# An expert loop's row gathers without an upper bound: empty slots read zero rows

## The chip, the cores and the metric

The kernel runs on one core of one Trainium2 chip. The metric is the device time in microseconds. Engines are called as in the profile: PE (TensorE), DVE (VectorE), ACT (ScalarE), POOL (GpSimd), SP (SyncE); sixteen DMA engines move the data.

## What is computed

One layer of a streaming encoder on 512 tokens of width 1024: attention, pooling, cross attention, then a mixture of 32 experts of which each token takes 4. Only the last part bears on the change:

```
logits = hf @ w_router + b_router
top_val, top_idx = top_k(logits, 4);  gates = softmax(top_val)
for each expert e, for its tokens:
    gu  = x @ w_gu[e] + b_gu[e]                      # 1024 -> 2048
    act = glu * sigmoid(1.702 * glu) * (lin + 1)      # glu, lin: clamped halves of gu
    y   = act @ w_down[e] + b_down[e]                 # 1024 -> 1024
    out[token] += gate * y
```

All data is fp32. Products are made from split operands (a high part and a low part of fp32r), so every weight unit of 128 x 2048 passes through ACT (high part, L1115) and DVE (low part, L1549) before PE uses it.

## The kernel before

The dense layers run first, to about 650 us. Then all 32 experts are served in turn. The first two are experts 0 and 1, the others follow by falling number of tokens. The first 17 blocks have 96 slots (`CAP`, heavy), the other 15 have 64 (`SLOTS_L`, light); tokens beyond that would go to extra blocks, which run in a loop at the end if there are any.

**Tables.** `hf_rows` in device memory holds the 512 normed token rows and behind them `CAP` = 96 rows of zeros. `slot_table` holds for each slot and block a token index and a gate. It starts with the index 512 + slot and the gate 0, so a slot that gets no token points at a zero row of its own. POOL fills in the tokens by indirect DMA (L772) and loads it as `slots`.

**The loop.** From turn 3 on light and heavy turns alternate. A turn i does the gate/up product of one expert and the down product of the one before it: 12 weight units of 1 MB (8 gate/up, 4 down), which SP loads into six raw buffers. SP waits for a buffer by `lo_done`, DVE's count of finished units. In order of use:

- SP: load unit (L480 gate/up, L487 down);
- ACT: high parts (L1115), and between them the copies of PSUM (`low`, L1145 and L1150; `ybuf`, L1157 and L1165), the gate (L1120) and the high parts of the activations;
- DVE: low parts (L1549), the clamp of the gate half (L1583, once in each turn), the clamp of the other half (L1585), their product (L1591);
- PE: gate/up products (L2273 heavy, L2219 light), down products (L2297, L2243), transposes of the gathered rows `xg` (L2175) and of the activations (L2184), and in light blocks the sums of shifted rows (L2191, L2198), which wait for ACT's `low`.

**POOL.** In each turn POOL issues one gather, for the expert whose gate/up product comes in the next turn: it waits until PE has turned the last rows out of `xg`, copies one column of `slots` to `idx_cur` (L670), and issues the indirect DMA (L675). Then it copies the index and gate column to `ycur` (L696), waits for `ybuf`, and issues the scatter that adds an expert's result rows to `moe_rows` (L702). Gather and scatter share POOL's DMA queue (q0). The scatter has a bound check too: an index above 511 is left out. The first three gathers of the program are written apart: L709 (twice) and L765 (once); their indices come from a product with a selection matrix, so an empty slot has index 0, and they have no bound. `xg` has 96 rows; a light block's gather fills the first 64. The last light turn also issues a gather for block 32, the first extra block.

Of the kernel before, what the change touches and what calls it, by code (L numbers as in the profile page):

```python
# [34 lines left out]
T = 512  # L35
# [127 lines left out]
def build(nc, A, out):  # L163
    with ExitStack() as ctx:
        def at(name, kb, shape, dt=F32):
            return nc.alloc_sbuf_tensor_at(name, shape, dt, offset=SB0 + int(kb * KB))
# [12 lines left out]
        def sem(name):  # L179
            return ctx.enter_context(nc.semaphore(name))  # L180
# [99 lines left out]
        def later(name, shape, dt=F32):  # L280
# [10 lines left out]
        idx_cur = at("idx_cur", 182.75, [CAP, 1], I32)  # L291
# [123 lines left out]
        idx_copied, gathered, x_turned, x_hi, x_ready = (  # L415
            sem(n) for n in ("idx_copied", "gathered", "x_turned", "x_hi", "x_ready"))
# [124 lines left out]
        def _(pool):  # L541
# [122 lines left out]
            def gather(block_column, copied, turned_before, n=CAP):  # L664


                pool.wait_ge(table_in, 16)

                pool.wait_ge(x_turned, turned_before)
                g.tensor_copy(idx_cur[:, :], slots[:, bass.ds(block_column, 1), 0]).then_inc(idx_copied, 1)  # L670

                pool.wait_ge(rows_filled, 16 * (TT + 2))
                pool.wait_ge(hf_stored, 16 * TT)
                pool.wait_ge(idx_copied, copied)
                g.indirect_dma_start(out=xg[0:n, :], out_offset=None, in_=hf_rows,  # L675
                                     in_offset=bass.IndirectOffsetOnAxis(ap=idx_cur[0:n, :], axis=0),
                                     bounds_check=T - 1, oob_is_err=False).then_inc(gathered, 16)

            def select(sel, e, ready, biased=None, used=None, n=CAP):

# [72 lines left out]
            for j in range(1, (T - 1 - SLOTS_L) // CAP + 1):  # L753
# [3 lines left out]
                if j < (T - 1 - SLOTS_L) // CAP:  # L757
# [8 lines left out]
                                 in_offset=bass.IndirectOffsetOnAxis(ap=idx_cur[:, :], axis=0)).then_inc(gathered, 16)  # L766
# [16 lines left out]
            select(sel_gu, third_expert, sel_gu_ready, gu_biased, 2)  # L783
            select(sel_dn, 1, sel_dn_ready, dn_biased, 1)
            gather(3, 2, 3, L)
            add_rows(0, 1)
            select(sel_dn, third_expert, sel_dn_ready, dn_biased, 2)

            def light_turn(i, first=False):
                e = expert_at(i)  # L790
                select(sel_gu_l, e, sel_gu_ready, gu_biased, i + 0, L)
                gather(i + 1, i + 0, i + 1)
                add_rows(i - 2, i - 1, 16 * i - 32, CAP if first else L)
                select(sel_dn_l, e, sel_dn_ready, dn_biased, i + 0, L)

            def heavy_turn(i):
                e = expert_at(i)
                select(sel_gu, e, sel_gu_ready, gu_biased, i + 0)
                gather(i + 1, i + 0, i + 1, L)
                add_rows(i - 2, i - 1, 16 * i - 32)  # L800
                select(sel_dn, e, sel_dn_ready, dn_biased, i + 0)
# [1572 lines left out]
```

## Time and profile before

| | |
|---|---|
| time, three runs | 1771.12, 1771.86, 1773.82 us; median 1771.86 |
| span of the profiled execution, first to last instruction | 1771.6 us, 22444 instructions |
| own time of the profiled execution | not listed apart; its span of 1771.6 us is within 0.3 us of the median of the runs |
| busy | PE 94%, PE weight load 74%, DVE 76%, ACT 63%, POOL 35% |
| mean granted clock of PE | 0.973 of full speed |
| data moved | 493.11 MB, of it 459.30 MB by SP's queue and 28.05 MB by POOL's |

The page cuts the span into 40 slices of 44.3 us. A digit is a busy share in tenths. The expert loop takes slices 17 to 39. A row of a timeline gives the start, the duration, the engine, the line and what it did; in square brackets stands the idle time before it and what ended that. In a row of windows the last three numbers are the granted PE clock (1.00 is full speed), the share of the sixteen DMA engines' time, and GB/s.

### The profile page before, as it was taken

How to read it: one execution, taken by the hardware profiler on the slowest of the kernel's cores; microseconds unless marked ns; L12 is line 12 of the kernel's file. 1: busy time of each engine (PE TensorE's matmuls, PEld its weight loads, DVE VectorE, ACT ScalarE, POOL GpSimd, SP SyncE). 2: the span in 40 equal slices, each digit the busy share in tenths (PEclk: the TensorE clock that was granted, in tenths of full speed). 3: DMA queues.
4: the chain of work that ended last, by engine and by line, in shares of the span. 5: the costliest groups of instructions: out<-in, count | busy, mean ns of one | idle time of the engine just before them, and what ended most of it. 6: DMA issues, size and time to landing. Idle time of an engine off the chain costs nothing.

```text
span 1771.6 us, 22444 instructions
## 1 busy us (share of the span) xinstructions
PE 1659.1 (94%) x7739; PEld 1309.1 (74%) x7739; DVE 1342.7 (76%) x1184; ACT 1121.9 (63%) x1030; POOL 614.6 (35%) x480
## 2 busy tenths in 40 slices
PE   6999999999989889999999999999999999999993
PEld 5877767889866677877777777777777777777772
DVE  5444563335433669999999999999999999999992
ACT  4134564234233245777887887887887887887882
POOL 5002231000000016345455455455454455455442
PEclk9999999999999989999999999999999999999996
DMA  9221222324431238999999999999999999999993
GB/s 316 104 95 60 76 68 83 126 95 143 166 98 48 77 132 303 397 393 383 393 389 398 396 394 397 395 394 397 394 392 395 392 396 396 389 394 397 388 377 105
DMA packets 110114, 493.11 MB, mean 278 GB/s; under 512 B 10461, under 2 KB 10530, under 8 KB 77194
## 3 DMA queue, kind: packets, MB, share of 16 engines
q1 hardware_dynamic: 98752, 459.30, 66.2%
q0 software_dynamic: 9824, 28.05, 6.0%
q10 hardware_dynamic: 1482, 5.01, 0.7%
q8 instruction: 35, 0.57, 0.1%
q14 instruction: 21, 0.17, 0.0%
HBM read 476.44 MB, written 20.38 MB: 280 GB/s over the span
## 4 chain that ended last, share of the span: by engine, by line
PE 39%; DVE 25%; issue 16%; DMA 12%; ACT 7%; POOL 0%; SPq 0%; DVEq 0%; ACTq 0%; POOLq 0%
DVE wlo L1549 18%; DMA raw<-in_w_gu 8%; PE ps L1820 7%; PE ps L1822 7%; PE ps L1821 7%; ACT whi L1115 4%; PE ps L2219 3%; DMA raw<-in_w_down 3%; PE ps L1943 2%; PE ps L1945 2%; PE ps L1947 2%; DVE glu L1583 1%; PE ps L2273 1%; PE ps L1970 1%; DVE lin L1585 1%
## 5 line engine op out<-in xcount | busy, mean ns | idle before, releaser
L1549 DVE TENSOR_TENSOR wlo<-raw,whi 128x2048 fp32r<-128x2048 f32 x380 | 846.9, 2282 | 44.5 <-ACT whi L1115 43.7
L1115 ACT ACTIVATE whi<-raw 128x2048 fp32r<-128x2048 f32 x380 | 714.6, 1912 | 101.7 <-DMA raw<-in_w_gu 51.4
L701 POOL TENSOR_TENSOR mark<-ident 1x1 f32<-1x1 f32 x32 | 160.2, 5007 | 380.1 <-ACT ybuf L1157 209.7
L1275 DVE TENSOR_TENSOR wlo<-raw,whi 128x2048 fp32r<-128x2048 f32 x52 | 120.0, 2331 | 145.6 <-ACT whi L847 145.6
L702 POOL DMA_INDIRECT moe_rows<-ybuf,ycur x32 | 174.4, 5450 | 6.3 <-issue 6.3
L2273 PE MATMUL ps<-whi,xhi 128*128 128x512 f32 x544 | 152.5, 403 | 0.6 <-DVE xlo L1554 0.3
L2273 PE MATMUL ps<-whi,xlo 128*128 128x512 f32 x544 | 146.4, 391 | 0.0
L2273 PE MATMUL ps<-wlo,xhi 128*128 128x512 f32 x544 | 146.4, 391 | 0.0
L847 ACT ACTIVATE whi<-raw 128x2048 fp32r<-128x2048 f32 x52 | 98.0, 1917 | 70.6 <-DVE branch L1426 30.2
L2219 PE MATMUL ps<-whi,xhl 128*128 128x512 f32 x480 | 134.8, 403 | 5.8 <-DVE xhl L1559 5.8
L2219 PE MATMUL ps<-wlo,xhl 128*128 128x512 f32 x480 | 134.4, 404 | 0.0
L2273 PEld LDWEIGHTS ps<-whi,xhi 128*128 128x128 f32 x544 | 101.7, 190 | 24.0 <-DVE wlo L1549 1.2
L2273 PEld LDWEIGHTS ps<-wlo,xhi 128*128 128x128 f32 x544 | 102.8, 189 | 21.9
L2273 PEld LDWEIGHTS ps<-whi,xlo 128*128 128x128 f32 x544 | 102.7, 189 | 21.7
L2219 PEld LDWEIGHTS ps<-whi,xhl 128*128 128x128 f32 x480 | 88.7, 190 | 30.7 <-issue 11.6
L2219 PEld LDWEIGHTS ps<-wlo,xhl 128*128 128x128 f32 x480 | 93.8, 196 | 20.6
L1120 ACT ACTIVATE glu<-glu 96x1024 f32<-96x1024 f32 (+1 forms) x32 | 33.9, 1061 | 92.1 <-DVE glu L1583 92.1
L2297 PE MATMUL ps<-whi,ahi 128*128 128x512 f32 x272 | 87.9, 405 | 0.0
L2297 PE MATMUL ps<-wlo,ahi 128*128 128x512 f32 x272 | 84.5, 392 | 0.0
L2297 PE MATMUL ps<-whi,alo 128*128 128x512 f32 x272 | 83.9, 390 | 0.0
L2243 PE MATMUL ps<-whi,ahl 128*128 128x512 f32 x240 | 76.9, 401 | 0.0
L2243 PE MATMUL ps<-wlo,ahl 128*128 128x512 f32 x240 | 73.9, 389 | 0.0
(383 smaller groups left out, 3020.7 us busy)
## 6 DMA issues: line engine op xcount, KB each, us to landing
raw<-in_w_gu SPq DMA_DIRECT2D x256, 1024.0 KB, 10.1
raw<-in_w_down SPq DMA_DIRECT2D x128, 1024.0 KB, 8.3
raw<-in_w_in SPq DMA_DIRECT2D x14, 1024.0 KB
raw<-in_w_gate SPq DMA_DIRECT2D x8, 1024.0 KB
raw<-in_w_xkv SPq DMA_DIRECT2D x8, 1024.0 KB
raw<-in_w_attn_up SPq DMA_DIRECT2D x4, 1024.0 KB
raw<-in_w_out SPq DMA_DIRECT2D x4, 1024.0 KB
raw<-in_w_xq SPq DMA_DIRECT2D x4, 1024.0 KB
```

Of the source, the lines that this page charges most:

```text
L701: g.tensor_tensor(mark[:, 0:1], ident[0:1, 0:1], ident[0:1, 1:2], ALU.add)
L702: g.indirect_dma_start(out=moe_rows, out_offset=bass.IndirectOffsetOnAxis(ap=ycur[0:n, 0:1], axis=0), in_=ybuf[0:n, :], in_offset=None, co ...
L1115: s.activation(his[m % DEPTH], raws[m % RAWS], ACT.Copy).then_inc(hi_done, 1)
L1275: v_.tensor_tensor(wlo[:, u % RING, :], raw[:, u % RING, :], whi[:, u % RING, :].bitcast(F32), ALU.subtract).then_inc(lo_done, 1)
L1549: v_.tensor_tensor(los[m % DEPTH], raws[m % RAWS], his[m % DEPTH].bitcast(F32), ALU.subtract).then_inc(lo_done, 1)
L1820: t_.matmul(dst, first[0], second[0], start=start, stop=False)
L1821: t_.matmul(dst, first[0], second[1], start=False, stop=False)
L1822: return t_.matmul(dst, first[1], second[0], start=False, stop=stop)
L2219: mm = t_.matmul(ps[:, n, :], xhl[:, k, :], w[:, n * 512:(n + 1) * 512], start=False, stop=False)
L2243: mm = t_.matmul(ps[:, 4 + n, :], ahl[:, k, :], w[:, c:c + 512], start=False, stop=False)
L2273: mm = t_.matmul(ps[:, n, :], a[:, k, :], w[:, n * 512:(n + 1) * 512], start=False, stop=k == KT - 1 and a is xlo)
L2297: mm = t_.matmul(ps[:, 4 + n, :], a[:, k, :], w[:, c:c + 512], start=False, stop=k == KT - 1 and a is alo)
```

## The change

The gathers in the loop lose their bound check. An index above 511 is no longer left out; the DMA reads the row of zeros at that index into `xg`. The three gathers ahead of the loop and the scatter stay as they are.

```
@@ gather(block_column, copied, turned_before, n=CAP)
                 g.indirect_dma_start(out=xg[0:n, :], out_offset=None, in_=hf_rows,
-                                     in_offset=bass.IndirectOffsetOnAxis(ap=idx_cur[0:n, :], axis=0),
-                                     bounds_check=T - 1, oob_is_err=False).then_inc(gathered, 16)
+                                     in_offset=bass.IndirectOffsetOnAxis(ap=idx_cur[0:n, :], axis=0)
+                                     ).then_inc(gathered, 16)
```

## Rows read from the trace of the kernel before

**Rows 1.** The page: slices of the DMA, and the scatter's group.

```profile
DMA  9221222324431238999999999999999999999993
GB/s 316 104 95 60 76 68 83 126 95 143 166 98 48 77 132 303 397 393 383 393 389 398 396 394 397 395 394 397 394 392 395 392 396 396 389 394 397 388 377 105
...
L702 POOL DMA_INDIRECT moe_rows<-ybuf,ycur x32 | 174.4, 5450 | 6.3 <-issue 6.3
```

**Rows 2.** Waits from 938.2 to 1071.3 us: total, times, longest.

```profile
DVE wlo L1549 <- ACT whi L1115: 6.3, 9, 2.5
...
ACT whi L1115 <- DMA raw<-in_w_gu: 5.7, 10, 1.3
```

**Rows 3.** Timeline of DVE: L1583 in eight turns.

```profile
792.49 1.21 DVE L1583 TENSOR_SCALAR glu<-ps 64x1024 f32<-64x1024 f32 x1
...
925.58 1.21 DVE L1583 TENSOR_SCALAR glu<-ps 64x1024 f32<-64x1024 f32 x1
...
1027.18 1.21 DVE L1583 TENSOR_SCALAR glu<-ps 96x1024 f32<-96x1024 f32 x1
...
1058.59 1.21 DVE L1583 TENSOR_SCALAR glu<-ps 64x1024 f32<-64x1024 f32 x1
...
1092.50 1.21 DVE L1583 TENSOR_SCALAR glu<-ps 96x1024 f32<-96x1024 f32 x1
...
1126.41 1.21 DVE L1583 TENSOR_SCALAR glu<-ps 64x1024 f32<-64x1024 f32 x1
...
1457.76 1.21 DVE L1583 TENSOR_SCALAR glu<-ps 64x1024 f32<-64x1024 f32 x1
...
1590.73 1.21 DVE L1583 TENSOR_SCALAR glu<-ps 64x1024 f32<-64x1024 f32 x1
```

**Rows 4.** Timelines of PE and ACT in two light turns; windows with PE's clock.

```profile
1038.28 0.67 PE L2191 MATMUL ps<-low,shift 128*64 128x512 f32 x2 [1.02 <-ACT low L1150]
...
1102.04 1.91 ACT L1115 ACTIVATE whi<-raw 128x2048 fp32r<-128x2048 f32 x1 [1.33 <-DMA raw<-in_w_gu]
...
1105.04 0.67 PE L2191 MATMUL ps<-low,shift 128*64 128x512 f32 x2 [2.45 <-ACT low L1150]
...
1039.00:1043.00 4.00, 4.00 (x24) 3.32 (x23) 4.00 (x3) 3.14 (x3) 0.00 (x0) 1.00 1.01 395
...
1106.00:1109.40 3.40, 3.40 (x13) 2.71 (x12) 2.71 (x3) 2.82 (x2) 0.00 (x0) 0.52 1.02 408
```

**Rows 5.** POOL's queue, 740-757, 776-790, 1118-1123, 1123-1130, 1700-1712 us: packets, MB, share.

```profile
q0 software_dynamic: 112, 0.23, 7.0%
...
q0 software_dynamic: 112, 0.21, 7.6%
...
q0 software_dynamic: 80, 0.24, 24.4%
...
q0 software_dynamic: 80, 0.24, 10.7%
...
q0 software_dynamic: 123, 0.00, 0.6%
```

**Rows 6.** POOL's queue over two stretches, 805.1-938.2 and 1470.4-1603.3 us.

```profile
q0 software_dynamic: 768, 2.39, 7.4%
...
q0 software_dynamic: 768, 1.89, 6.0%
```

**Rows 7.** The gathers by line (ns min/median/max), landing, one issue, PE's use.

```profile
L675 POOL DMA_INDIRECT xg<-hf_rows,idx_cur x30: 1019/1348/3020, 724.9 to 1695.1; - x30
...
DMA to landing us min/median/max: 7.2/8.7/10.0
...
L709 POOL DMA_INDIRECT xg<-hf_rows,first_idx x2: 934/1018/1103, 656.2 to 662.4; - x2
...
1093.54 1.03 POOL L675 DMA_INDIRECT xg<-hf_rows,idx_cur  x1 [0.91 <-POOL idx_cur L670]
...
1118.04 0.88 PE L2175 MATMUL ps<-ident,xg 96*128 96x96 f32 x8
```

## The prediction

> **What bounds the kernel now.** I read the page first [rows 1]. The gathers in question run from 724.9 to 1695.1 us [rows 7], in the expert loop, and there every slice has the DMA engines at 9 tenths and about 395 GB/s. On the same page PE, DVE and ACT stand at 7 to 9 tenths in these slices; such a page names no bound, so the next view is the waits of one stretch of four turns (two light, two heavy) [rows 2]. In 133.1 us ACT waits 5.7 us for gate/up weights to land and DVE waits 6.3 us for ACT. So weights do arrive late at some places, and more DMA traffic could cost time.
>
> The third view is the start of L1583, once in each turn [rows 3]. From 1027.18 to 1058.59 one turn takes 31.41 us; from 1092.50 to 1126.41 the same kind of turn (light) takes 33.91. The pattern repeats every four turns, and the four-turn period is what I cost the change against. The two light turns differ by 2.50 us, and [rows 4] shows why. In the slow one ACT waits 1.33 us for a gate/up unit (1102.04), so its copy of `low` (L1150) is late, PE pauses 2.45 us at L2191, and in the stretch right behind the pause the granted clock is 0.52, that is the lower level, 1.2 GHz; in the quick one PE pauses 1.02 us and the clock stays at 1.00. So the loop is one closed cycle of DMA, ACT, PE and clock; a late weight unit is paid for in every second light turn.
>
> **What the change touches.** Before, a slot without a token holds the index 512 + slot; the bound is 511, so the gather leaves that row out. After, the index is legal (the table has 608 rows) and a row of 4,096 bytes is read. How does a left-out row look now? The last gather of the loop, at 1695.1 us, is for the expert behind the 32nd and has 96 empty slots: from 1700 to 1712 us the pool queue shows 123 packets and 0.00 MB [rows 5]. So a left-out row is a tiny packet, 0.6% of 16 engines in 12 us over 123 packets = 9.4 ns of one engine.
>
> How many rows are added? Blocks 0 to 16 have 96 slots and the 15 others 64: 2,592 slots. Tokens fill 512 x 4 = 2,048 of them (the page has 32 scatters by L702 [rows 1], so no token went to an extra block); 544 are empty. The first three gathers (L709, L765) have no bound already. The scatters of the first two experts move 0.23 and 0.21 MB [rows 5], 56 and 51 rows of 96, so 40 + 45 empty slots lie there; the third expert is the fullest of the rest and I count it full. That leaves 459 rows, and the 96 of the last gather: 555 rows, 2.27 MB, 0.5% of the page's 493 MB.
>
> The price of one row. From 1123 to 1130 us the pool queue holds one light gather alone: 80 packets, 0.24 MB (59 rows), 10.7% of 16 engines in 7 us = 11.98 us of one engine; less 21 tiny packets, 200 ns per row [rows 5]. Added per row: 200 - 9 = 191 ns of one engine, or 11.9 ns of all sixteen. The dearest row of this size in the trace is the scatter's, 24.4% of 5 us for 59 rows, 331 ns, or 20.1 ns of all sixteen [rows 5]; I take the gather's since it is the same operation, and keep the other for the range. If nothing hides them: 459 x 11.9 = 5.5 us (9.2 at the scatter's price), and 96 x 11.9 = 1.1 us for the last gather. The lower bound is nothing.
>
> How much passes through to the span? The trace holds an experiment on this already, since experts are served by falling load. From 805.1 to 938.2 us the pool queue moved 2.39 MB, from 1470.4 to 1603.3 only 1.89 MB [rows 6]: 0.50 MB or 122 rows fewer, half gathered and half scattered. Unhidden that would be 61 x 11.9 + 61 x 20.1 = 1.95 us. The four turns took 925.58 - 792.49 = 133.09 us and 1590.73 - 1457.76 = 132.97 us [rows 3]: 0.12 us, a share of 6%. Four turns hold 640 slots, gathered and scattered together, so 57 to 179 are empty in these stretches, half of them gathered: after the change each moves 28 to 90 rows more, so its pool traffic lies mostly inside what the loop has carried already (461 to 583 rows), and the first two or three stretches lie up to 40 rows above it. By the share of 6% the 459 rows cost 0.3 us; since that share is unproven above 583 rows I take twice this, 0.6 us. What hides the rest is the other work of the cycle: most of ACT's waits for weights fall where DVE is still busy with earlier units. If this cover were gone the cost would be the 5.5 us above.
>
> The last gather is counted at nothing too: its data lands in `xg`, which nobody reads, and all that it can delay is the last few down units, which pass through at the same 6%. Without that cover it is 1.1 us, in the range.
>
> Is a gather itself late? It takes 7.2 to 10.0 us from issue to landing [rows 7]. The one issued at 1093.54 is in `xg` by about 1103.5; PE turns it (L2175) at 1118.04: 14.5 us to spare, against some 0.3 us for 20 to 30 more rows. Nor is POOL late: on it ycur (L696) stands behind the gather and waits for the scatter before it anyway. On POOL the gather takes a median of 1348 ns with the bound against 934 to 1103 without (L709) [rows 7]. I count that at nothing: its results have the 14.5 us, and the fastest bounded one took 1019 ns too. If it were on the path it would be worth up to 30 x 0.33 = 10 us, which is the faster rival's room.
>
> The sum: the profiled execution's span is 1771.6 us, the runs' median 1771.86. 1771.86 + 0.6 = 1772.5 us.
>
> **A rule of the skill against it.** The Trainium skill, DMA: Bandwidth & Descriptors, section Specifications, gives about 358 GB/s as what HBM gives one core. By it this loop is over its limit already and every byte must cost: an estimate from that page is 2.27 MB / 358 GB/s = 6.3 us. The trace disagrees, with slices of 395 GB/s and more [rows 1], and the measurement decides; yet that the traffic has no headroom is just what the first rival says in rows.
>
> **Rivals.** *A, the DMA is the bound and every added row counts.* For it: DMA share full in every slice of the loop, ACT's waits for weights. Against it: the 0.12 us where 1.95 were due. It gives 5.5 us, 1777.3; with the last gather or the dearer price up to 1781. It decides once the pool queue moves more than the cycle carries, and only the first stretches go past what was seen.
>
> *B, the cycle tips to the slow turn.* If the added rows (up to 31 in one gather, 0.4 us) delay weights in the quick light turns as well, PE's pause there grows from 1.02 to 2.4 us, the clock falls there too, and each costs 2.50 us more. There are 7 such turns, one between each two slow ones and one behind: 1771.9 + 17.5 = 1789.4 us. The point is a weight unit 1.3 us later than now, and 122 rows more or fewer did not move the pattern. One such turn more would be 2.5 us, still inside 0.2%. The Trainium skill, TensorE: Matmul & The Clock Gate, section What's actually happening, says that the default state is throttled and that activity releases it; the clock after the long pause agrees.
>
> *C, faster.* A gather without the bound check leaves POOL up to 0.3 us sooner, so its packets and the scatter's are over before the unit on which ACT waits at 1102.04. If that wait goes, so do the long pause and the low clock: 7 slow light turns in the loop (one in 133 us, from 838 to 1638 us), each 2.50 us, 17.5 us in all, 1754. The point is the whole wait of 1.33 us; against it, the gather ahead of that wait took 1.03 us as it is [rows 7], and its rows grow.
>
> *D, nothing changes in the queue*, because the zero rows are left out in some other way: 1771.9, inside the forecast.
>
> **How the numbers follow.** This kernel tells 0.2% (3.5 us) from no change. Forecast with D 0.70 (1772.5, own range 1770.5 to 1775), A 0.16, B 0.07, C 0.07. A and B end slower, C faster; of the forecast's 0.70 a hundredth each way falls outside 0.2%. So faster 0.08, same 0.68, slower 0.24. The range takes in the forecast's spread and A at the gather's price: 1770.2 to 1777.6, leaving out B, C and the dear end of A.
>
> **What would show it.** Pool queue: the packets over the loop stay the same in number, 2.3 MB more, the tiny ones gone where the gathers are; the last gather shows 0.39 MB. L1583 four turns apart: 133.0 to 133.3 us; A says 133.4 to 134.1. PE's pauses at L2191 still alternate between 1.0 and 2.4 us; B and C say that they don't. Wrong would be the prediction if the pattern of pauses changes, or if a gather's row is much dearer than 200 ns, as all gathers then read the same few rows.

## The result, and the profile after

The changed kernel takes 1778.73 us (median of 5 runs, 1775.6 to 1780.46), the kernel before 1771.86 (5 runs). The ratio is 1.0033 with a 95% interval from 1.0020 to 1.0046, that is 5.8 us slower (3.5 to 8.1). The forecast was 1772.5 us, range 1770.2 to 1777.6, with 0.68 on no difference. The time lies outside the range, on the side and near the size of rival A.

How many rows were added can be read from the page alone, in the line of packets. First the line of the kernel before:

```profile
DMA packets 110114, 493.11 MB, mean 278 GB/s; under 512 B 10461, under 2 KB 10530, under 8 KB 77194
```

And the slices, packets and queues of the changed kernel's page, which answer to [rows 1]:

```profile
span 1777.5 us, 22414 instructions
...
DMA  9221212324431238999999999999999999999993
GB/s 323 95 95 60 79 65 84 124 95 142 166 98 48 85 139 305 396 389 384 397 389 398 401 387 398 396 391 401 395 393 401 395 392 398 400 389 389 402 361 104
DMA packets 110114, 495.37 MB, mean 279 GB/s; under 512 B 9909, under 2 KB 9978, under 8 KB 77194
```

The packets are as many as before, but 10461 - 9909 = 552 tiny ones have become rows, and the data has grown by 2.26 MB. The rate in the loop (slices 17 to 39) is about what it was: 384 to 402 GB/s, with one slice of 361, against 377 to 398 before. More bytes at the same rate is what a loop bound by its transfers looks like; the experiments below say how far that holds.

The timeline of DVE has the starts of L1583, which answer to [rows 3]:

```profile
793.15 1.21 DVE L1583 TENSOR_SCALAR glu<-ps 64x1024 f32<-64x1024 f32 x1
...
926.77 1.21 DVE L1583 TENSOR_SCALAR glu<-ps 64x1024 f32<-64x1024 f32 x1
...
1060.54 1.21 DVE L1583 TENSOR_SCALAR glu<-ps 64x1024 f32<-64x1024 f32 x1
...
1460.66 1.21 DVE L1583 TENSOR_SCALAR glu<-ps 64x1024 f32<-64x1024 f32 x1
...
1595.07 1.21 DVE L1583 TENSOR_SCALAR glu<-ps 64x1024 f32<-64x1024 f32 x1
...
1694.99 1.21 DVE L1583 TENSOR_SCALAR glu<-ps 96x1024 f32<-96x1024 f32 x1
...
1729.02 1.21 DVE L1583 TENSOR_SCALAR glu<-ps 64x1024 f32<-64x1024 f32 x1
```

Over four turns that is 133.62, 133.77 and 134.41 us; the prediction had 133.0 to 133.3, and rival A 133.4 to 134.1. For the last two turns the kernel before has:

```profile
1692.20 1.21 DVE L1583 TENSOR_SCALAR glu<-ps 96x1024 f32<-96x1024 f32 x1
...
1723.04 1.21 DVE L1583 TENSOR_SCALAR glu<-ps 64x1024 f32<-64x1024 f32 x1
```

Set side by side, the 5.9 us between the two spans lie in these places:

| stretch | before | after | difference |
|---|---|---|---|
| up to the start of the loop's pattern | 792.49 | 793.15 | 0.66 |
| from there to the last full turn | 899.71 | 901.84 | 2.13 |
| the last turn, in which the empty last gather lands | 30.84 | 34.03 | 3.19 |
| behind it, to the end of the span | 48.53 | 48.43 | -0.10 |

So more than half is in one turn. These are two single executions. In the runs that list both, the span is 1.7 to 1.9 us less than the time, so the one before took some 1773.4 us, which is over its median. The 2.13 us of the second row are less sure than they look: with the last gather's rows alone added (below), where the loop up to there is that of the kernel before, the same stretch takes 898.20 us, 1.51 less than before. The last turn is steadier, as shown below. Here are PE and ACT of the changed kernel in that turn, and a window behind PE's pause:

```profile
1704.68 1.91 ACT L1115 ACTIVATE whi<-raw 128x2048 fp32r<-128x2048 f32 x1 [1.49 <-DMA raw<-in_w_gu]
...
1707.69 0.83 PE L2191 MATMUL ps<-low,shift 128*64 128x512 f32 x2 [2.67 <-ACT low L1150]
...
1708.00:1711.40 3.40, 3.40 (x10) 2.66 (x9) 2.71 (x2) 3.37 (x2) 0.00 (x0) 0.51 1.02 410
```

The kernel before had no wait for weights there, a pause of 1.03 us and the full clock. In the changed kernel a gate/up unit comes 1.49 us late, PE pauses 2.67 us and the clock falls to its lower level. What took the DMA's time is in the queue. From 1700 to 1712 us, where [rows 5] has 123 packets with 0.00 MB and 0.6% of the engines' time, the pool queue of the changed kernel has:

```profile
q0 software_dynamic: 112, 0.39, 10.4%
```

That is the last gather: 96 rows, 208 ns of one engine each. In the other turns the pattern of pauses is no longer strict, which the prediction had named as a sign of being wrong. Two of the long ones are shorter, one comes in a turn that was quick before (1573.70), and the turn behind it, slow before, is quick (1639.79):

```profile
972.51 0.68 PE L2191 MATMUL ps<-low,shift 128*64 128x512 f32 x2 [1.83 <-ACT low L1150]
...
1506.21 0.67 PE L2191 MATMUL ps<-low,shift 128*64 128x512 f32 x2 [1.66 <-ACT low L1150]
...
1573.70 0.68 PE L2191 MATMUL ps<-low,shift 128*64 128x512 f32 x2 [2.42 <-ACT low L1150]
...
1639.79 0.68 PE L2191 MATMUL ps<-low,shift 128*64 128x512 f32 x2 [0.98 <-ACT low L1150]
```

The gather itself has become shorter on POOL and is in time, as [rows 7] had it before:

```profile
L675 POOL DMA_INDIRECT xg<-hf_rows,idx_cur x30: 950/958/3024, 725.4 to 1695.9; - x30
...
DMA to landing us min/median/max: 7.4/8.4/10.3
```

The step from a median of 1348 ns to 958 is not the price of the check. In the run with the last gather's rows alone the check is there as before, and the median is 1029:

```profile
L675 POOL DMA_INDIRECT xg<-hf_rows,idx_cur x30: 1014/1029/3027, 724.2 to 1692.9; - x30
```

The shortest gathers take 1012 to 1019 ns with the check in all but two of the runs, and 947 and 950 in the two without it. So the check takes POOL about 0.07 us; the medians of the runs with it lie anywhere from 1028 to 1737 ns.

### The profile page after: what moved, and what is told of

Its sections match the earlier page's. It is cut to its first block, busy times and chain, and to the rows that moved or that the text cites. A ratio compares the mean times of both kernels' runs of the same rounds, so it can differ in the third digit from the quotient of the medians.

```text
span 1777.5 us, 22414 instructions
## 1 busy us (share of the span) xinstructions
PE 1661.1 (93%) x7739; PEld 1309.1 (74%) x7739; DVE 1344.0 (76%) x1184; ACT 1123.0 (63%) x1030; POOL 599.2 (34%) x480
## 2 busy tenths in 40 slices
DMA packets 110114, 495.37 MB, mean 279 GB/s; under 512 B 9909, under 2 KB 9978, under 8 KB 77194
## 4 chain that ended last, share of the span: by engine, by line
PE 36%; DVE 24%; issue 16%; DMA 14%; ACT 8%; ACTq 0%; POOL 0%; DVEq 0%; SPq 0%; POOLq 0%
DVE wlo L1549 17%; DMA raw<-in_w_gu 9%; PE ps L1820 7%; PE ps L1821 7%; PE ps L1822 7%; ACT whi L1115 5%; DMA raw<-in_w_down 4%; PE ps L1943 2%; PE ps L1945 2%; PE ps L1947 2%; DVE glu L1583 2%; PE ps L2219 1%; PE ps L2273 1%; PE ps L1970 1%; DVE lin L1585 1%
## 5 line engine op out<-in xcount | busy, mean ns | idle before, releaser
L702 POOL DMA_INDIRECT moe_rows<-ybuf,ycur x32 | 170.1, 5316 | 6.1 <-issue 6.1
L2219 PEld LDWEIGHTS ps<-wlo,xhl 128*128 128x128 f32 x480 | 93.8, 195 | 20.6
L1120 ACT ACTIVATE glu<-glu 96x1024 f32<-96x1024 f32 (+1 forms) x32 | 33.9, 1060 | 88.6 <-DVE glu L1583 88.6
```

The source lines that it names most:

```text
L702: g.indirect_dma_start(out=moe_rows, out_offset=bass.IndirectOffsetOnAxis(ap=ycur[0:n, 0:1], axis=0), in_=ybuf[0:n, :], in_offset=None, co ...
L2219: mm = t_.matmul(ps[:, n, :], xhl[:, k, :], w[:, n * 512:(n + 1) * 512], start=False, stop=False)
```

## Experiments

All were timed against the kernel before, each on the same chip as it. Differences in us are the ratio's, times 1771.

**The check or the rows?** One number of the kernel before decides which indices are left out, so the number of rows can be set while the instructions and the number of packets stay (110,114; at a bound of 0 one register move of POOL less per gather).

```
-                                     bounds_check=T - 1, oob_is_err=False).then_inc(gathered, 16)
+                                     bounds_check=T + CAP - 1, oob_is_err=False).then_inc(gathered, 16)
```

> The kernel before with the bound at 607 instead of 511: the check stays, but every zero row is read, 552 rows or 2.26 MB more, as in the changed kernel. Theory T1 (the rows cost: the loop is at the limit of its DMA) and theory T2 (rows beyond what the loop's cycle carries cost, rows fewer gain little) both expect the changed kernel's time, 1776 to 1780 us. Theory T3 (the missing check costs, by the timing of POOL's instructions) expects the time of before, 1771 to 1773.

Measured: 1.0033 (1.0020 to 1.0046), 1777.41 us. That is the changed kernel's ratio to the last digit. With the check and all the rows the time is that of the changed kernel: the rows make the difference, and the missing check shows no effect within these intervals of some 2.3 us either way.

**Other numbers of rows.** The same number at 575 (`T + SLOTS_L - 1`), 383, 255 and 0. The last three leave out rows of tokens too, so those kernels don't compute the whole result.

> The bound at 575: of the empty slots those below 64 are read, that is all of the light blocks (159 rows in the loop) and 64 of the last gather; the heavy blocks' empty slots stay out. T1 expects 159 x 11.9 ns = 1.9 us and up to 0.8 for the last gather: 1773.8 to 1774.6. T2 expects between 0 and 1 us, 1772 to 1773, since the pool queue then stays within what the loop had carried already in all but the first stretch. T3 expects the time of before.

> The bound at 383: a quarter of the token rows of the loop's gathers is left out, some 460 rows less; those slots keep stale rows, so the output is not the reference's. T1 expects 460 x 11.9 ns = 5.5 us less than before, and on the line through the runs with 928 and 1,845 rows less 6 to 7 us less. A staircase, in which the slow turn's pause stays until it goes at once, expects 0 to 2 us less, with the whole step between this and 928 rows less.

> The bound at 255: about half of the token rows are left out of the loop's gathers too, some 930 rows or 3.8 MB less than before, with as many packets and instructions. Those slots keep stale rows, so the output is not the reference's. T1 expects 930 x 11.9 ns = 11 us less, about 1761. T2 expects within 2 us of before. T3 expects the time of before.

> The bound at 0: nearly all rows of the loop's gathers are left out, some 1,850 rows or 7.6 MB less than before, with as many packets and instructions; the slots keep stale rows, so the output is not the reference's. T1 expects 1,850 x 11.9 ns = 22 us less, about 1750, until another engine becomes the bound. T2 expects within 3 us of before, or a step down of up to 17 us if the long pauses and the low clock of the slow light turns go. T3 expects the time of before.

| bound | rows against before | ratio (95%) | us |
|---|---|---|---|
| 575 | +223 | 1.0047 (1.0035 to 1.0059) | +8.3 |
| 383 | -463 | 0.9977 (0.9964 to 0.9989) | -4.1 |
| 255 | -928 | 0.9919 (0.9907 to 0.9932) | -14.3 |
| 0 | -1,845 | 0.9860 (0.9846 to 0.9874) | -24.8 |

The theory that more rows cost and fewer gain little (T2) falls with the bounds of 255 and 0. The kernel before was already paying for its gathered rows: from -1,845 to +552 rows the time rises by 30.6 us, 12.8 ns per row on average, and the prediction's 11.9 ns is near that. It isn't an even slope, though: 9 ns per row for the first 463 fewer, 22 for the next 465. And 223 rows cost, by the middle value, more than 552 (6.2 to 10.4 us against 3.5 to 8.1, so the intervals overlap); every theory had expected 3 us or less for them.

The run with bound 0 reaches a floor. Here are two starts of L1583 four turns apart, and the windows row of the loop:

```profile
986.27 1.21 DVE L1583 TENSOR_SCALAR glu<-ps 64x1024 f32<-64x1024 f32 x1
...
1115.29 1.21 DVE L1583 TENSOR_SCALAR glu<-ps 64x1024 f32<-64x1024 f32 x1
...
930.00:1590.00 660.00, 650.07 (x3032) 510.73 (x3031) 644.02 (x349) 551.42 (x350) 380.72 (x142) 1.00 1.01 398
...
ACT whi L1115 <- DMA raw<-in_w_gu: 6.6, 13, 0.6
```

The period is 129.02 us and stays within 0.03 of that all through the loop; DVE is busy for 644.02 of 660 us. The DMA share still reads 1.01, as in the kernel before. So that number can't tell a loop bound by its transfers from one that isn't. ACT's wait for gate/up units does: 6.6 us here against this, in the same window of the kernel before, where the wait for down units stands beside it:

```profile
ACT whi L1115 <- DMA raw<-in_w_gu: 29.7, 53, 1.3
ACT whi L1115 <- DMA raw<-in_w_down: 27.7, 50, 0.7
```

It tells the two apart but does not measure how far the loop is from the floor: it is 35.1 us with 463 rows fewer and 27.5 with 928 fewer. The wait for down units tells less (20.6 us at bound 0). The room also lies in one kind of turn only. At the floor the turn from a start of L1583 with 96 rows to the next with 64 takes 30.9 us and the other kind 33.6; in the kernel before the first kind takes 31.4 to 33.9 within the loop, and the other one 33.6 to 34.2.

**Which rows?** Light blocks' gathers, heavy blocks', and the last one alone, by a bound of their own (here the light ones):

```
-            def gather(block_column, copied, turned_before, n=CAP):
+            def gather(block_column, copied, turned_before, n=CAP, bound=T - 1):
...
-                gather(i + 1, i + 0, i + 1, L)
+                gather(i + 1, i + 0, i + 1, L, T + CAP - 1)
```

> The kernel before with the bound at 607 for the light blocks' gathers alone: 159 rows more, at most 32 in one gather. T1 (each row costs its share of the DMA, 11.9 ns, wherever it lies) expects 1.9 us over before. A theory T4, formed after the bound of 575 cost more than the bound of 607 with fewer rows: the light gathers lie ahead of the unit on which the slow turn waits, and their rows cost several times their share; it expects 5 to 8 us over before.

> The bound at 607 for the heavy blocks' gathers alone, without the last gather of the loop: 297 rows more, 10 to 31 in one gather. T1 expects 3.5 us over before. T4 expects 0 to 2 us over before, or less time than before, since this part would have to take back some of the light gathers' cost in the changed kernel.

> The bound at 607 for the last gather of the loop alone, whose 96 rows nobody reads. T1 expects 1.1 us over before; if the last down units are late in any case already, up to that; if they have slack, nothing. T4 expects nothing.

> The bound at 607 for all gathers of the loop but the last: 456 rows more than before. If the parts add up, 6.0 + 1.9 = 7.9 us over before, more than the changed kernel. If each row costs one share of the DMA, 5.4 us. If the last gather makes 3.4 us of the changed kernel's 5.9, 2.5 us.

| with a bound of 607 | rows | ratio (95%) | us | ns per row |
|---|---|---|---|---|
| light | 159 | 1.0034 (1.0021 to 1.0047) | +6.0 | 38 |
| heavy | 297 | 1.0011 (1.0002 to 1.0019) | +1.9 | 7 |
| last | 96 | 1.0019 (1.0010 to 1.0027) | +3.4 | 35 |
| light and heavy | 456 | 1.0017 (1.0006 to 1.0028) | +3.0 | 7 |

The parts do not add up: light and heavy together cost less than light alone by its middle value, though the intervals overlap (1.1 to 5.0 us against 3.7 to 8.3). The runs with the bound of 575 and of 607 show the same once more: the light rows and two thirds of the last gather's come to 8.3 us, as their parts add up to (6.0 + 2.3), and all rows to 5.8. What stands is that all rows but the last gather's cost 3.0 us, about half of their 5.4 us share, and that the last gather makes up the rest of the changed kernel's 5.8 us. The profiles point the same way. This is the last turn of the run without the last gather's rows, then of the run with them alone, with ACT's two longest waits for weights in its last turn:

```profile
1691.95 1.21 DVE L1583 TENSOR_SCALAR glu<-ps 96x1024 f32<-96x1024 f32 x1
...
1722.83 1.21 DVE L1583 TENSOR_SCALAR glu<-ps 64x1024 f32<-64x1024 f32 x1
```

```profile
1689.97 1.21 DVE L1583 TENSOR_SCALAR glu<-ps 96x1024 f32<-96x1024 f32 x1
...
1722.14 1.21 DVE L1583 TENSOR_SCALAR glu<-ps 64x1024 f32<-64x1024 f32 x1
...
1703.92 1.92 ACT L1115 ACTIVATE whi<-raw 128x2048 fp32r<-128x2048 f32 x1 [0.96 <-DMA raw<-in_w_gu]
...
1721.62 1.92 ACT L1115 ACTIVATE whi<-raw 128x2048 fp32r<-128x2048 f32 x1 [1.89 <-DMA raw<-in_w_down]
```

30.88 us without, 32.17 with. Over all profiles with L2191 in its old place the last turn takes 30.8 to 30.9 us wherever the last gather reads nothing, and 32.2, 33.3, 33.9 and 34.0 us where it reads its 64 or 96 rows. These rows are wanted by nobody, but they come just ahead of the last weight units. In the run with them alone the last turn shows 1.3 us of the 3.4 measured; where the rest lies a single profile can't say, since what follows the last start of L1583 takes 46.9 to 50.5 us in the profiles without these rows.

The run with the last gather alone shows one thing more. Up to 1690 us it runs the instructions and rows of the kernel before, and yet these are starts of L1583 four turns apart in its trace:

```profile
1358.02 1.22 DVE L1583 TENSOR_SCALAR glu<-ps 96x1024 f32<-96x1024 f32 x1
...
1490.36 1.21 DVE L1583 TENSOR_SCALAR glu<-ps 96x1024 f32<-96x1024 f32 x1
...
1624.61 1.21 DVE L1583 TENSOR_SCALAR glu<-ps 96x1024 f32<-96x1024 f32 x1
```

132.34 and 134.25 us. The steady 133.0 of the one profile before, from which the prediction read an effect of 0.12 us, is one way among several in which this loop can run.

**Do PE's pauses and the low clock carry the cost?** The matmuls on which PE pauses come two weight units later:

```
-                    if k == 3 and sums_before is not None:
+                    if k == 5 and sums_before is not None:
                         shift_sums(sums_before)
```

> The kernel before with the two matmuls of L2191, for which PE pauses 1.0 or 2.4 us, moved behind two more weight units (k == 5 instead of k == 3); the gathers keep their bound and no bytes change. If the DMA alone sets the loop's pace (T1), the long pauses go, the clock stays at its upper level, and yet the time falls only to what the bytes need: four turns move 52.5 MB, at the 398 GB/s of the run with bound 255 that is 131.9 us instead of 133.05, 8 us over the loop. If the pause and the low clock behind it are a cost of their own (T5), each slow light turn gains its 2.5 us: 17 us over the loop, about 1754. If neither holds, within 2 us of before.

> The changed kernel with the matmuls of L2191 at k == 5, where they make no long pause. Against the kernel before with the same move (1.0004 of before) it has the 552 rows more. T1 (the DMA sets the pace, each row costs its 11.9 ns) expects 5.5 to 6.6 us over that, 1776 to 1777.5, with the clock at its upper level all through the loop. T5 (the pauses and the low clock carry the change's cost) expects no more than 2 us over it.

> The kernel with the light gathers' 159 rows added, 1.0034 of before, with the matmuls of L2191 at k == 5. T1 expects 1.9 us over before: without the long pauses the light rows cost their share. T4 (rows ahead of the unit on which the slow turn waits cost several times their share, by the position alone) expects 5 to 8 us over before here too.

> The heavy gathers' 297 rows added, with the matmuls of L2191 at k == 5. One share per row expects 3.5 us over before. A theory by position (light rows dear, heavy rows cheap) expects 0 to 2 us.

> The last gather's 96 rows added, with the matmuls of L2191 at k == 5. One share per row expects 1.1 us over before, a tail with slack nothing, a place where the rows are dear 3 us or more.

> The bound at 255, some 928 rows less than before, with the matmuls of L2191 at k == 5; the slots keep stale rows, so the output is not the reference's. With the sums at 3 this was 14.4 us less. If 11.9 ns per row is the whole cost it is 11 us less than the kernel before with the sums at 5. If the low clock and the long pauses added to the 14.4 us, the difference between the two places of the sums is 2 us or more here; if the DMA is all, there is none.

| rows | sums at 3, us (95%) | sums at 5, us (95%) |
|---|---|---|
| as before | 0 | +0.7 (-0.9 to 2.1) |
| all, +552 | +5.8 (3.5 to 8.1) | +5.0 (3.2 to 6.7) |
| light, +159 | +6.0 (3.7 to 8.3) | +3.0 (1.4 to 4.8) |
| heavy, +297 | +1.9 (0.4 to 3.4) | +1.8 (0.2 to 3.2) |
| last, +96 | +3.4 (1.8 to 4.8) | +1.9 (0.4 to 3.4) |
| bound 255, -928 | -14.3 (-16.5 to -12.0) | -13.6 (-15.9 to -11.5) |

Timeline and window of the kernel before with the sums at 5:

```profile
1107.50 0.63 PE L2191 MATMUL ps<-low,shift 128*64 128x512 f32 x2
...
930.00:1590.00 660.00, 637.93 (x2945) 494.19 (x2945) 630.25 (x337) 543.38 (x338) 336.70 (x140) 1.00 1.01 396
...
ACT whi L1115 <- DMA raw<-in_w_gu: 37.2, 69, 1.3
...
ACT whi L1115 <- DMA raw<-in_w_down: 21.4, 41, 0.6
```

No pause, the full clock over the whole window, and no time gained. ACT's waits for gate/up and down units together are 58.6 us against 57.4 before, and the rate is 396 GB/s against 395. Neither theory had its gain: T5 expected 17 us less and T1 in the form given there 8 us less. What came is the third case, within 2 us of before. T5 falls. It falls with the changed kernel too, where it expected no more than 2 us over the kernel before with the same move, and 4.3 came (5.0 - 0.7). So taking away the pauses and the low clock gains nothing here; that they are idle time of a loop that waits for its transfers, in another shape, is the reading that fits, though no run shows what the move costs by itself. With the bound at 255 the gain against the kernel before with the same move is 14.3 us, as it was with the sums at 3, so that gain is not the clock's either. T4, by which the light rows are dear by their place alone, expected 5 to 8 us for them here and got 3.0. Against the kernel before with the same move the parts come to 2.3 (light), 1.1 (heavy) and 1.2 us (last), 4.6 in all against the 4.3 measured together: here they add up by the middle values, as they did not with the sums at 3. The intervals are too wide to call this shown.

The Trainium skill, TensorE: Matmul & The Clock Gate, section Terms, puts the penalty of throttled time at that time x (1 - K/N); for the loop's seven stretches of some 3.4 us at half clock that is an estimate of 12 us. The trace shows the low clock (0.52 and 0.51 in the windows behind two long pauses), but no such cost: the run without it takes the same time, within -0.9 to 2.1 us.

**What does a scattered row cost?** The bound of the scatter (L704) at 607, 255 and 0.

> The kernel before with the scatter's bound at 607 and the gathers' as they are: 544 rows more are added into the rows behind the tokens, each 331 ns of one engine by the record. If these records are work of the DMA (T1 as the prediction priced it) that is 544 x 20.1 ns = 10.9 us over before. If a scatter's row waits for memory in its record while other traffic goes on, it costs well under a gather's row, 0 to 5 us, and then the fewer rows of the late stretches, half of them scattered, could not show in the period.

> The scatter's bound at 255: about half of the 2,048 scattered rows are left out, so the output lacks part of the experts' sums. If a scattered row costs what a gathered one does (928 gathered rows fewer gave 14.4 us), about 15 us less than before. If it costs 3 ns, as the 544 rows behind the tokens did, 3 us less. At the 20.1 ns of the prediction, 20 us less.

> The kernel before with the scatter's bound at 0: nearly all of the 2,048 scattered rows are left out, with as many packets and instructions, so the output lacks the experts' part. At the 20.1 ns per row of the prediction this is 41 us less, as far as another engine allows (the run with 1,845 gathered rows less stopped at 24.7). If a scattered row costs 3 ns, as the run with the scatter unbounded says, it is about 6 us less. If it costs a gathered row's 12 to 13 ns, 24 us less.

| scatter bound | rows | ratio (95%) | us | ns per row |
|---|---|---|---|---|
| 607 | +544 | 1.0009 (1.0000 to 1.0019) | +1.6 | 3 |
| 255 | -1,024 | 0.9976 (0.9967 to 0.9985) | -4.3 | 4 |
| 0 | -2,044 | 0.9853 (0.9840 to 0.9865) | -26.0 | 13 |

A scattered row takes 331 ns in the records against a gathered one's 200, and I priced it at 20.1 ns of the span. Near the working point it costs 3 to 4. The last run is at the same floor as the gathers' bound of 0 (the profile's starts of L1583):

```profile
990.70 1.21 DVE L1583 TENSOR_SCALAR glu<-ps 64x1024 f32<-64x1024 f32 x1
...
1119.73 1.21 DVE L1583 TENSOR_SCALAR glu<-ps 64x1024 f32<-64x1024 f32 x1
```

129.03 us. So between 1,024 and 2,044 rows fewer each row was worth 21 ns or more by the middle values, as between 463 and 928 gathered ones. No one price fits both bounds: by the expectations a gathered row's price gave 15 us for 255 and 24 for 0, and 3 ns gave 3 and 6, against 4.3 and 26.0 measured.

## Why the prediction was wrong

**Right.** The rows: 555 counted, 552 found (the third expert, counted as full, has 3 empty slots). The kind of cost: DMA time, not POOL's, not the check's, and no late gather (7.4 to 10.3 us to land, as before). The price of a gathered row in the records: 200 ns, 208 in the changed kernel, though the zero rows are the same 96 for all its gathers. The faster rival, that the check's time on POOL mattered, is out: the run that kept the check took the same time as the one without, and the check takes 0.07 us per gather, not the 0.33 that the prediction read from a median, so its room was 2 us and not 10. B came about in part: of its seven quick light turns two became slow in the profile (1573.70, and the last one at 1707.69), while one slow turn became quick, and the count of low-clock stretches in the loop is seven, as before. Its 17.5 us did not come, and with the sums at 5, where no such stretch is left, the rows still cost 4.3 us.

**The step that failed first** is "The last gather is counted at nothing too". It was given a cost only as a bound, 1.1 us. It measured 3.4 us alone (1.8 to 4.8), and in the changed kernel's profile the last turn is 3.2 us longer. That nobody reads its data says nothing on who waits behind it: ACT has 13 or 14 weight units still to take when it is issued. No other gather adds as many rows at once (32 at most), and the delay of one unit also set off PE's long pause; with the sums at 5, without that pause, these rows cost 1.2 us over the kernel with the same move. That there is no later turn to make the delay good is an argument; no run issued this gather at another place.

**The second** is "By the share of 6% the 459 rows cost 0.3 us", and its double, 0.6. The 456 rows measured 3.0 us (1.1 to 5.0), some 55% of their share. The comparison of two stretches from which the 6% came had two faults that runs show. Half of its 122 rows were scattered ones, which I priced at 20.1 ns; by the scatter's runs they cost 3 to 4, so not 1.95 us were due but about 61 x 11.9 + 61 x 4 = 1.0 us. And the 0.12 us found was no measurement: the same loop has periods of 132.34 and 134.25 us in another execution. An effect of 1 us can't be read from two periods of one profile.

**A premise was wrong too**, "a late weight unit is paid for in every second light turn". Without the pauses and the low clock the time was the same, so they carry no cost of their own that these runs could see. Rival A had it right, and its 5.5 us, with 1.1 for the last gather, come to within a microsecond of the 5.8 measured. But it is right in the sum more than in the parts: the loop's rows cost half their share, and the last gather's three times theirs. The 0.16 that it got was too little. The evidence for it, waits of ACT for weights [rows 2], was a direct one, and the wait for down units, as long again (27.7 us against 29.7 in 660), was left out of it; the evidence against it was a difference of two numbers.

**Open.** Why rows are dear in one place and cheap in another. With the sums at 3 the heavy gathers' rows cost 7 ns, the light ones' 38 and the last one's 35; with the sums at 5, against the kernel before with the same move, 4, 14 and 13. Part of that may be PE's pause, since the light and the last rows are cheaper without it, but the intervals are wide. That 159 light rows alone cost, by the middle value, more than 456 of both kinds is not explained. Nor is the bend, by which the second half of the rows taken away is worth more than twice the first. Empty slots are the last ones of a block and a lower bound leaves out the last slots first, so the rows in question may not be spread evenly over the sixteen engines; no run changed the order of slots, and the profile gives only the mean over the engines. None of the kernels that compute the whole result is faster than the kernel before, so that one stays.

## What to carry to other kernels

Take the waits of the consumers for their data as the sign that transfers bound a loop, and price added bytes at about their full share then, with room on both sides: it gave the right sum here, but 0.6 of it for the loop's rows, three times it for the last gather's, and a sixth for scattered rows near the working point. A DMA share of 1.0 was no evidence for or against: it read 1.01 on the floor too. Look at work behind which the last units of a loop stand, even if its result is not used. A comparison of two stretches within one trace needs the spread of such stretches first, from a second execution, and rows of one kind only.

## What was not expected of the hardware

- A row that a bound leaves out still makes a packet: 110,114 packets in both kernels, 552 of them tiny before and rows of 4,096 bytes after.
- The bound check itself costs POOL about 0.07 us per gather by the shortest ones (1012 to 1019 ns against 947 and 950), and the kernel nothing that shows. The medians of the same gathers with the check range from 1028 to 1737 ns between runs, so one trace's median does not price it.
- A scattered, accumulated row is recorded with 331 ns and costs the kernel 3 to 4 ns near its working point; a gathered one with 200 to 208 ns costs 4 to 38, by its place and run.
- With PE's pauses taken away the clock stayed at its upper level for the whole loop, and the time did not change (1.0004, 0.9995 to 1.0012).
